# Root sums of the grouped norm computed inside the attention, tokens on partitions

## Chip, cores and metric

The kernel runs on one core of a Trainium2 chip. The metric is the device time in microseconds of the execution.

## What is computed

One layer of a hybrid model on 576 tokens: 512 of a prompt and 8 sequences of 8 sampled tokens. A projection of the normed input gives z, the convolution input, the step sizes, q, k, v and two gates. A state-space scan and a windowed attention with sinks run on them, their outputs are gated, merged and projected, and a product-key expert network follows. The change concerns the norm of the scan's output, by groups of 256 channels (8 groups), for each token:

```
y = y.reshape(bsz, l, SSM_D_INNER) * jax.nn.silu(z.astype(f32))
yg = y.reshape(bsz, l, SSM_N_GROUPS, SSM_D_INNER // SSM_N_GROUPS)
yg = yg * lax.rsqrt(jnp.mean(yg * yg, axis=-1, keepdims=True) + NORM_EPS)
y = (yg.reshape(bsz, l, SSM_D_INNER) * lw['ssm_norm_w'].astype(f32)).astype(z.dtype)
return y @ lw['w_ssm_out'], conv_new, ssm_new.astype(ssm_prev.dtype)
```

The attention itself does not need this norm, nor does the norm need the attention. Both are needed by the merge behind them.

## The kernel before

Activations lie with channels on the 128 partitions and the 576 tokens along the row (T = 576, HT = 288). Five engines run programs of their own and meet in semaphores. Each weight tile of 128 output channels (1024 x 128, 512 KB) is handled in order everywhere: SyncE loads it into `raw`, ScalarE's `high` rounds it into `whi` (L1380), GpSimd's `low` subtracts to give `wlo` (L632), and TensorE multiplies three times (hi x hi, hi x lo, lo x hi), here in `project` (L733, both token halves, 48 matmuls) or `gate_raw` (L958, one half, 24 matmuls).

Stages that matter here, by time of the trace: the scan and z (to about 550 us), q, k and v (to 628), the attention (628 to 794), the projection of the attention output with the grouped norm beside it (795 to 865), the projection of the scan's output (from 865), and the rest.

The attention has UA = 20 units: 16 of the prompt (4 token chunks by 4 key heads) and 4 of the samples. The orders are written out by hand, one list for each engine:

- TensorE, for u = 0 to 19: `turn(u)` (L1063, waits for the normalised weights), `scores(u + 2)` (L1046), `gate_half(u)`, then `values(u)` (L1090; L1077 and L1079 for samples). `gate_half(u)` is half a weight tile of the output gates, unrelated to the attention, one half tile in every unit. It waits in `ga_used` until ScalarE has copied half tile u - 1 out of bank 7.
- ScalarE: `take(u)` (L1593, L1594), `weights(u + 2)` (L1581, the exponentials), `store_gate(u)` (L1602 copies the half tile into `rinv`, L1604 sends it to memory). Where u is odd, `store_gate` ends in `high` for the weight tile that `gate_half(u + 3)` needs.
- VectorE: `back(u + 1)` (L2196 to L2199), `take` of two units together where u is even (L2218, L2219), `front(u + 2)` (L2182, L2158 to L2162), which ends in the maxima that `weights(u + 2)` waits for.
- GpSimd: `low` for each weight tile, one for two units.

In the next stage there are 8 projections. Around each, one group of the norm is done: ScalarE squares two tiles (`z_square`, L1633), TensorE multiplies them with a 128 x 128 matrix of ones, which leaves the sum of squares on all 128 partitions (`group_sums`, L1124), ScalarE takes the root of 128 x 576 elements (`z_std`, L1640), VectorE takes the reciprocal (`yn`, L2244), scales the two tiles (L2248) and splits them (L2257, L2258). Between, `att` (L1887) applies the attention's gate. TensorE's order is `group_sums(0)`, tile 0, `group_sums(1)`, tile 1, and so on.

Of the kernel before, what the change touches and what calls it, by code (L numbers as in the profile page):

```python
# [22 lines left out]
F32 = mybir.dt.float32  # L23
# [7 lines left out]
P = 128  # L31
# [176 lines left out]
def build(nc, xT, wt, pu, pv, consts, params, subk, conv_in, ropes, amask, smask, s_in, kct, kc, vc,  # L208
# [3 lines left out]
    act_dram = nc.dram_tensor("activations", [ET, P, DT], F32).ap()  # L212
    ga_dram = nc.dram_tensor("gates_raw", [GS_E + GT_N, P, T], F32).ap()
# [3 lines left out]
    with ctx:  # L217
# [53 lines left out]
        RW = put(misc, "row_weight", [P, ROWS])  # L271
        tmp_at = misc[0]
# [85 lines left out]
        SQZ = [nc.alloc_sbuf_tensor_at(f"sqz{i}", [P, T], F32, offset=conv_at + 2304 * i) for i in range(2)]  # L358

# [52 lines left out]
        def sem(name):  # L412
# [8 lines left out]
        abc_in = [sem(f"abc_in{i}") for i in range(4)]  # L421
        acum_copied, acum_out, e2_in, e2_ready = [
            sem(n) for n in ("acum_copied", "acum_out", "e2_in", "e2_ready")]
# [23 lines left out]
        dt_v, dt_abs, dt_exp, dt_ready, dtt_ready, dtk_ready = [  # L447
            sem(n) for n in ("dt_v", "dt_abs", "dt_exp", "dt_ready", "dtt_ready", "dtk_ready")]
# [12 lines left out]
        rs_ready, rope_done, v_ready, v_turned, v_tok = [  # L461
            sem(n) for n in ("rs_ready", "rope_done", "v_ready", "v_turned", "v_tok")]
# [7 lines left out]
        zs_ready, yz_ready, zsq_ready, zsq_used, zstd, yn_done = [  # L470
            sem(n) for n in ("zs_ready", "yz_ready", "zsq_ready", "zsq_used", "zstd", "yn_done")]
# [19 lines left out]
        def _(sp):  # L491
# [17 lines left out]
            def load_rows(u):  # L509

                c, g = divmod(u, NG)
                src = acum_dram[c:c + 1, 4 * g:4 * g + 4, :].to_broadcast([P, 4, P])
                sp.dma_start(ABC[u % 4][:, :, :], src).then_inc(abc_in[u % 4], 16)

            def load_rows_sample(s):

                if s < 2:
# [3 lines left out]
                    .then_inc(abc_in[s], 16)  # L521
# [14 lines left out]
            sp.wait_ge(acum_out, 16 * NC)  # L536
# [88 lines left out]
        def _(pool):  # L625
# [71 lines left out]
            with pool.Fori((N_QKV + 3) // 2, N_GU // 2) as i:  # L697
                for k in range(2):
                    low(Idx(k, i, 2))
# [20 lines left out]
        def _(pe):  # L720
# [407 lines left out]
            group_sums(0, first=True)  # L1128
            pe.wait_ge(o_done, UNITS // 2 + SB // 2)
            for k in range(2):  # L1130
                project(Idx(N_ATT + k), Idx(P_ATT + k), OH, OL)
                group_sums(k + 1)
            with pe.Fori(1, KD // 2 - 1) as i:
                for k in range(2):
                    project(Idx(N_ATT + k, i, 2), Idx(P_ATT + k, i, 2), OH, OL)
                    group_sums(i * 2 + (k + 1))
            for k in range(2):
                project(Idx(N_ATT + KD - 2 + k), Idx(P_ATT + KD - 2 + k), OH, OL)
                if k == 0:
                    group_sums(KD - 1)  # L1140
# [200 lines left out]
        def _(act):  # L1341
# [105 lines left out]
            for c in range(NC):  # L1447
                t0, L = chunk(c)
                act.dma_start(acum_dram[c, :, 0:L], ACT_[:, t0:t0 + L]).then_inc(acum_out, 16)
# [27 lines left out]
            def exps(u):  # L1477
# [3 lines left out]
                act.wait_ge(abc_in[u % 4 if u < PU else g // 2], 16 * (u // 4 + 1 if u < PU else NG + 1))  # L1481
# [114 lines left out]
            def store_gate(u):  # L1596
# [3 lines left out]
                act.wait_ge(ga_out[h], 16 * (GS_E + m))  # L1600
                cut = RINV[:, h * HT:(h + 1) * HT]
# [1114 lines left out]
```

## Time and profile before

| | us |
|---|---|
| runs | 2532.62, 2545.24, 2552.91 |
| median | 2545.24 |
| span of the profiled execution | 2530.3 |
| TensorE busy | 2409.4 (95%) |
| VectorE busy | 1780.0 (70%) |
| ScalarE busy | 1077.0 (43%) |
| GpSimd busy | 886.8 (35%) |

The span runs from the first to the last instruction of one execution. The profile names no separate time for that execution, so the runs stand beside it: the fastest is 2.3 us above the span, the median 14.9 us. In the rows, PE is TensorE, PEld its weight loads, DVE VectorE, ACT ScalarE, POOL GpSimd. The busy shares are means over stages that differ; the rows below come from the two stages of the change. PEclk is the granted clock of TensorE, 1.00 being 2.4 GHz and 0.50 being 1.2 GHz.

### The profile page before, as it was taken

How to read it: one execution, taken by the hardware profiler on the slowest of the kernel's cores; microseconds unless marked ns; L12 is line 12 of the kernel's file. 1: busy time of each engine (PE TensorE's matmuls, PEld its weight loads, DVE VectorE, ACT ScalarE, POOL GpSimd, SP SyncE). 2: the span in 40 equal slices, each digit the busy share in tenths (PEclk: the TensorE clock that was granted, in tenths of full speed). 3: DMA queues.
4: the chain of work that ended last, by engine and by line, in shares of the span. 5: the costliest groups of instructions: out<-in, count | busy, mean ns of one | idle time of the engine just before them, and what ended most of it. 6: DMA issues, size and time to landing. Idle time of an engine off the chain costs nothing.

```text
span 2530.3 us, 44965 instructions
## 1 busy us (share of the span) xinstructions
PE 2409.4 (95%) x15016; PEld 2231.8 (88%) x15016; DVE 1780.0 (70%) x3445; ACT 1077.0 (43%) x2049; POOL 886.8 (35%) x504
## 2 busy tenths in 40 slices
PE   7999779999799999899999999999999999999997
PEld 6999659989678999899998899899899999999996
DVE  6655775543664822377999887788568888888887
ACT  3554763335554522133343677777532222222222
POOL 1333364433111343244455543444423331222221
PEclk8999999999998999999999999999999999999998
DMA  3222344432211323133444788899999999999994
GB/s 140 75 82 75 110 136 158 156 116 84 78 58 62 100 88 121 58 106 121 143 153 146 247 325 318 301 345 355 339 324 317 321 314 307 311 312 310 310 309 148
DMA packets 271272, 498.46 MB, mean 197 GB/s; under 512 B 138000, under 2 KB 176912, under 8 KB 270096
## 3 DMA queue, kind: packets, MB, share of 16 engines
q1 hardware_dynamic: 71472, 228.49, 26.7%
q10 hardware_dynamic: 162816, 134.23, 16.3%
q0 software_dynamic: 36864, 134.23, 15.2%
q8 instruction: 63, 1.03, 0.2%
q14 instruction: 57, 0.47, 0.1%
HBM read 421.13 MB, written 76.93 MB: 197 GB/s over the span
## 4 chain that ended last, share of the span: by engine, by line
PE 57%; issue 23%; DVE 10%; POOL 4%; ACT 3%; DMA 2%; ACTq 1%; DVEq 0%; POOLq 0%; SPq 0%
PE ps L1295 24%; PE ps L1190 14%; PE ps L733 9%; PE ps L918 5%; POOL wlo L632 4%; PE ps L1260 3%; DMA raw<-wt 1%; DVE seg L2035 1%; PE ps L886 1%; DVE onehot_pick L2420 1%; ACT whi L1380 1%; PE ps L901 1%; ACT rinv L1778 1%; DVE expert_parts L2426 1%; DVE onehot_pick L2423 1%
## 5 line engine op out<-in xcount | busy, mean ns | idle before, releaser
L1380 ACT ACTIVATE whi<-raw 128x1024 fp32r<-128x1024 f32 x373 | 394.4, 1058 | 1069.9 <-PE ps L1295 452.9
L632 POOL TENSOR_TENSOR wlo<-raw,whi 128x1024 fp32r<-128x1024 f32 x177 | 439.0, 2481 | 842.2 <-ACT whi L1380 842.2
L1190 PE MATMUL ps<-h_hi,whi 128*128 128x448 f32 x1024 | 381.3, 372 | 5.8 <-DVE wlo L2481 4.9
L1190 PE MATMUL ps<-h_hi,wlo 128*128 128x448 f32 x1024 | 375.5, 367 | 0.0
L1190 PE MATMUL ps<-h_lo,whi 128*128 128x448 f32 x1024 | 375.3, 367 | 0.0
L1295 PE MATMUL ps<-act_hi,whi 128*128 128x448 f32 x1000 | 365.2, 365 | 0.0
L1295 PE MATMUL ps<-act_lo,whi 128*128 128x448 f32 x1000 | 365.2, 365 | 0.0
L1295 PE MATMUL ps<-act_hi,wlo 128*128 128x448 f32 x1000 | 365.2, 365 | 0.0
L2481 DVE TENSOR_TENSOR wlo<-raw,whi 128x1024 fp32r<-128x1024 f32 x196 | 240.3, 1226 | 157.2 <-ACT whi L1380 142.8
L643 POOL DMA_INDIRECT row<-pv,row_idx x128 | 166.2, 1298 | 465.8 <-DVE row_acc L2509 442.1
L643 POOL DMA_INDIRECT row<-pu,row_idx x128 | 185.8, 1451 | 251.4 <-DVE row L2472 231.9
L1190 PEld LDWEIGHTS ps<-h_hi,whi 128*128 128x128 f32 x1024 | 193.2, 189 | 23.1 <-issue 5.0
L1190 PEld LDWEIGHTS ps<-h_hi,wlo 128*128 128x128 f32 x1024 | 192.9, 188 | 16.5
L1190 PEld LDWEIGHTS ps<-h_lo,whi 128*128 128x128 f32 x1024 | 193.2, 189 | 15.1
L1295 PEld LDWEIGHTS ps<-act_hi,wlo 128*128 128x128 f32 x1000 | 187.8, 188 | 14.9
L1295 PEld LDWEIGHTS ps<-act_lo,whi 128*128 128x128 f32 x1000 | 187.8, 188 | 14.9
L1295 PEld LDWEIGHTS ps<-act_hi,whi 128*128 128x128 f32 x1000 | 187.8, 188 | 14.9
L733 PE MATMUL ps<-h_hi,whi 128*128 128x288 f32 x832 | 181.7, 300 | 11.6 <-POOL wlo L632 11.6
L733 PE MATMUL ps<-h_hi,wlo 128*128 128x288 f32 x832 | 180.4, 299 | 0.0
L733 PE MATMUL ps<-h_lo,whi 128*128 128x288 f32 x832 | 180.2, 299 | 0.0
L2509 DVE SCALAR_TENSOR_TENSOR row_acc<-row,row_weight,row_acc 128x1024 f32<-128x1024 f32 x128 | 163.7, 1279 | 0.5 <-DVE row_acc L2509 0.3
L2472 DVE SCALAR_TENSOR_TENSOR row<-row,h_rows 128x1024 f32<-128x1024 f32 x128 | 151.8, 1220 | 3.0 <-DMA row<-pu,row_idx 3.0
(344 smaller groups left out, 4773.7 us busy)
## 6 DMA issues: line engine op xcount, KB each, us to landing
raw<-wt SPq DMA_DIRECT2D x245, 512.0 KB
raw<-pv SPq DMA_DIRECT2D x128, 512.0 KB
activations<-tmp ACTq DMA_DIRECT2D x128, 224.0 KB
gates_dense<-g_block ACTq DMA_DIRECT2D x7, 4096.0 KB
g_tile<-gates_dense ACTq DMA_DIRECT2D x128, 224.0 KB
gelu<-activations ACTq DMA_DIRECT2D x128, 224.0 KB
a_cum_rows<-decay_sums SPq DMA_DIRECT2D x32, 256.0 KB, 3.1
state_s<-s_in SPq DMA_DIRECT2D x16, 512.0 KB, 6.0
```

The source lines that it names most:

```text
L632: pool.tensor_tensor(lo, raw[n.par][:, :], hi.bitcast(F32), ALU.subtract).then_inc(split_ready, 1)
L643: pool.indirect_dma_start(GR[b][:, :], None, table[:, :], bass.IndirectOffsetOnAxis(ap=IDX[:, s:s + 1], axis=0))\
L733: mm = pe.matmul(PS[2 * p.par + h][:, 0:HT], w[slot][:, k, :], x[:, k0 + k + (l0 if x is xl else 0), h * HT:(h + 1) * HT], start=first and ...
L886: mm = pe.matmul(bank(PU + g)[:, lo:lo + SL], S0[v % 8][:, b, :], UBS[:, NG + g, SL * b:SL * (b + 1)], start=True, stop=True)
L918: mm = pe.matmul(PS[2 + h][:, 0:HT], w[slot][:, k, :], x[:, k, h * HT:(h + 1) * HT], start=k == 0 and i == 0, stop=k == KD - 1 and i == 2)
L1190: mm = pe.matmul(PS[2 * p.par][:, 0:DT], w[slot][:, k, :], x[:, k, 0:DT], start=k == 0 and w is whi and x is HH, stop=k == KD - 1 and w is ...
L1260: mm = pe.matmul(out, OJ[k][:, q, :], AI[k][:, q, :], start=True, stop=True)
L1295: mm = pe.matmul(PS[d][:, 0:DT], w[s][:, d, :], x[b][:, :], start=first and w is whi and x is ACH, stop=False)
L1380: act.activation(whi[slot][:, :, :].rearrange("p k c -> p (k c)"), raw[slot][:, :], ACT.Copy)\
L2472: dve.scalar_tensor_tensor(row[:, :], row[:, :], 1.0, HS[:, :], ALU.mult, ALU.mult, accum_out=dot).then_inc(row_used, 1)
L2481: dve.tensor_tensor(lo, raw[slot][:, :], hi.bitcast(F32), ALU.subtract).then_inc(split_ready, 1)
L2509: dve.scalar_tensor_tensor(ACCS[:, :], GR[b][:, :], w, ACCS[:, :], ALU.mult, ALU.add).then_inc(row_used, 1)
```

## The change

Squares, sums and roots move into the attention. After `store_gate(u)`, for u = 0 to 15, ScalarE squares one tile. GpSimd adds the two squares of a group behind its `low` of that pair of units. TensorE, ahead of `gate_half(2g + 2)`, multiplies the sum (as the stationary operand, 5 chunks of 128 tokens) with one column of ones, so the sums of all groups come out as 5 x 8 columns with tokens on partitions, in the free part of bank 7. At unit 17 one root of 128 x 40 elements is taken, VectorE takes one reciprocal, and after the attention TensorE turns the 40 columns into rows. ScalarE copies them and sends them to memory in 5 DMAs; from there each group's row comes back, repeated over 128 partitions, by one DMA into one of two buffers (`RB`). In the projection stage the sums of TensorE, the roots of ScalarE and the wide reciprocals of VectorE are gone. Two semaphores are renamed (`abc_in` to `bcast_in`, `acum_out` to `rows_out`).

```diff
+    zinv_dram = nc.dram_tensor("group_roots", [NG, T], F32).ap()
...
+        ZINV = put(misc, "group_root", [P, NC, NG])
+        ZROW = put(misc, "group_root_rows", [NC * NG, P])
...
+        RB = [nc.alloc_sbuf_tensor_at(f"group_rinv{i}", [P, T], F32, offset=conv_at + 2304 * i) for i in range(2)]
...
-            with pool.Fori((N_QKV + 3) // 2, N_GU // 2) as i:
+            with pool.Fori((N_QKV + 3) // 2, (N_GT + 1) // 2) as i:
+                for k in range(2):
+                    low(Idx(k, i, 2))
+            low(Idx(N_GT + 1))
+            for g in range(NG):
+                low(Idx(N_GT + 2 + g))
+                pool.wait_ge(zsq_ready, 2 * g + 2)
+                pool.tensor_tensor(SQZ[1][:, :], SQZ[1][:, :], SQZ[0][:, :], ALU.add).then_inc(zsq_added, 1)
+            low(Idx(N_GT + 2 + NG))
+            with pool.Fori((N_GT + 3 + NG) // 2, N_GU // 2) as i:
                 for k in range(2):
                     low(Idx(k, i, 2))
...
+                if u % 2 == 0 and 0 < u <= 2 * NG:
+                    group_sum(u // 2 - 1)
                 gate_raw(Idx(N_GT + m), h, PS[3 if u == GA_AT else 7], (ga_half, tile_done)[h])
+
+            def group_sum(g):
+
+                pe.wait_ge(zsq_added, g + 1)
+                for c in range(NC):
+                    t0 = min(c * P, T - P)
+                    mm = pe.matmul(PS[7][:, HT + NG * c + g:HT + NG * c + g + 1], SQZ[1][:, t0:t0 + P], ONES[:, 0:1],
+                                   start=True, stop=True)
+                mm.then_inc(zsq_used, 1)
 
             gate_half(GA_AT)
             pe.wait_ge(v_tok, 1)
@@ -1114,30 +1138,15 @@
...
+            pe.wait_ge(zinv_ready, 1)
+            pe.transpose(PS[4][0:NC * NG, 0:P], ZINV[:, :, :].rearrange("p c g -> p (c g)"), ident).then_inc(pt_ready, 1)
             pe.wait_ge(sc_used, UA)
-            def group_sums(g, first=False):
-                pe.wait_ge(zsq_ready, g * 2 + 2)
-                if not first:
-                    pe.wait_ge(zstd, g)
-                for k in range(2):
-                    for h in range(2):
-                        mm = pe.matmul(PS[4 + h][:, 0:HT], ONES[:, :], SQZ[k][:, h * HT:(h + 1) * HT],
-                                       start=k == 0, stop=k == 1)
-                    mm.then_inc(zsq_used, 1)
-
-            group_sums(0, first=True)
             pe.wait_ge(o_done, UNITS // 2 + SB // 2)
             for k in range(2):
                 project(Idx(N_ATT + k), Idx(P_ATT + k), OH, OL)
-                group_sums(k + 1)
-            with pe.Fori(1, KD // 2 - 1) as i:
+            with pe.Fori(1, KD // 2) as i:
                 for k in range(2):
                     project(Idx(N_ATT + k, i, 2), Idx(P_ATT + k, i, 2), OH, OL)
-                    group_sums(i * 2 + (k + 1))
-            for k in range(2):
-                project(Idx(N_ATT + KD - 2 + k), Idx(P_ATT + KD - 2 + k), OH, OL)
-                if k == 0:
-                    group_sums(KD - 1)
...
+                if u == UA - 3:
+                    act.wait_ge(zsq_used, NG)
+                    act.activation(ZINV[:, :, :].rearrange("p c g -> p (c g)"), PS[7][:, HT:HT + NC * NG], ACT.Sqrt, bias=Q[:, Q_EPS:Q_EPS + 1],
+                                   scale=float(NG) / INNER).then_inc(zstd, 1)
...
+            def z_square(g, k):
+
+                if g == 0:
+                    act.wait_ge(rope_done, 10)
+                    act.wait_ge(yz_ready, CI)
+                elif k == 0:
+                    act.wait_ge(zsq_added, g)
+                else:
+                    act.wait_ge(zsq_used, g)
+                act.activation(SQZ[k][:, :], at(UX, g * 2 + k), ACT.Square).then_inc(zsq_ready, 1)
...
+                if u < CI:
+                    z_square(u // 2, u % 2)
...
-            def z_square(g, k, first=False):
-                if not first:
-                    act.wait_ge(zsq_used, g * 2 + (k - 1))
-                act.activation(SQZ[k][:, :], at(UX, g * 2 + k), ACT.Square).then_inc(zsq_ready, 1)
-
-            def z_std(g, first=False):
-                act.wait_ge(zsq_used, g * 2 + 2)
-                if not first:
-                    act.wait_ge(y_scaled, g)
-                for h in range(2):
-                    ins = act.activation(RINV[:, h * HT:(h + 1) * HT], PS[4 + h][:, 0:HT], ACT.Sqrt,
-                                         bias=Q[:, Q_EPS:Q_EPS + 1], scale=float(NG) / INNER)
-                ins.then_inc(zstd, 1)
-
+            def rinv_back(g, k):
+
+                act.dma_start(RB[k][:, :], zinv_dram[g:g + 1, :].to_broadcast([P, T]) if isinstance(g, int) else
+                              zinv_dram[bass.ds(g, 1), :].to_broadcast([P, T])).then_inc(bcast_in[k], 16)
+
+            act.wait_ge(pt_ready, UA + 1)
+            act.activation(ZROW[:, :], PS[4][0:NC * NG, 0:P], ACT.Copy).then_inc(pt_copied, 1)
+            act.wait_ge(pt_copied, UA + 1)
+            for c in range(NC):
+                t0, L = chunk(c)
+                act.dma_start(zinv_dram[:, t0:t0 + L], ZROW[c * NG:(c + 1) * NG, P - L:P]).then_inc(rows_out, 16)
...
-                z_std(m, first=first and k == 0)
                 if not (first and k == 0):
                     high(plus(n, 1))
                 if not (last and k):
-                    for j in range(2):
-                        z_square(m + 1, j)
                     if not (first and k == 0):
+                        act.wait_ge(y_scaled, m)
+                        rinv_back(m + 1, 1 - k)
                         p = plus(p, -1)
                         act.wait_ge(slot_used[p.par], p.half + 1)
                     gate_back(m + (GS_B + 1), 1 - k)
...
+            act.wait_ge(rows_out, 16 * 2 * NC)
             for k in range(2):
-                z_square(0, k, first=True)
+                rinv_back(k, k)
...
+                if u == UA - 2:
+                    dve.wait_ge(zstd, 1)
+                    dve.reciprocal(ZINV[:, :, :], ZINV[:, :, :]).then_inc(zinv_ready, 1)
...
-            def yn(g, yh):
-                dve.wait_ge(zstd, g + 1)
-                own.link(dve.reciprocal(RINV[:, :], RINV[:, :]))
+            def yn(i, b, yh):
+                g = i * 2 + b
+                dve.wait_ge(bcast_in[b], i * 16 + 16 * (NG + 2))
                 for k in range(2):
                     y = at(UX, g * 2 + k)
                     m = g * 2 + k
                     ins = dve.scalar_tensor_tensor(y, y, Q[:, bass.ds(m + Q_SNW, 1)],
-                                                   RINV[:, :], ALU.mult, ALU.mult)
+                                                   RB[b][:, :], ALU.mult, ALU.mult)
```

## Rows read from the trace of the kernel before

**Rows 1.** Windows of stages: us, busy by engine (instructions), PEclk, DMA share, GB/s.

```profile
688.00:703.00 15.00, 13.04 (x98) 10.44 (x97) 10.01 (x21) 8.00 (x26) 2.40 (x1) 1.00 0.16 56
748.00:760.00 12.00, 12.00 (x142) 10.07 (x141) 8.59 (x25) 7.38 (x20) 3.26 (x2) 1.00 0.26 82
806.30:864.50 58.20, 58.20 (x394) 55.23 (x392) 54.67 (x62) 42.20 (x54) 16.00 (x7) 1.00 0.28 85
```

**Rows 2.** Timeline of TensorE in the attention: start, us, operation, [idle before].

```profile
695.39 0.40 PE L958 MATMUL ps<-h_hi,whi 128*128 128x288 f32 x1 [1.65 <-ACT rinv L1602]
...
702.26 0.40 PE L958 MATMUL ps<-h_hi,whi 128*128 128x288 f32 x1 [0.31 <-ACT rinv L1602]
...
705.61 1.08 PE L1090 MATMUL ps<-p_turned,v_tok 128*64 128x256 f32 x8
...
707.65 1.14 PE L1046 MATMUL ps<-k_pad,q 64*128 64x256 f32 x8
...
747.39 0.40 PE L958 MATMUL ps<-h_hi,whi 128*128 128x288 f32 x1 [0.54 <-ACT rinv L1602]
...
759.45 0.40 PE L958 MATMUL ps<-h_hi,whi 128*128 128x288 f32 x1
```

**Rows 3.** Timeline of ScalarE in the attention.

```profile
701.82 0.39 ACT L1602 ACTIVATE rinv<-ps 128x288 f32<-128x288 f32 x1
...
702.68 1.06 ACT L1380 ACTIVATE whi<-raw 128x1024 fp32r<-128x1024 f32 x1 [0.47 <-ACT rinv L1602]
...
707.92 0.51 ACT L1581 ACTIVATE scores<-scores,att_small 128x256 f32<-128x256 f32 x1 [3.22 <-DVE att_small L2162]
```

**Rows 4.** Timeline of GpSimd in the attention.

```profile
703.81 2.40 POOL L632 TENSOR_TENSOR wlo<-raw,whi 128x1024 fp32r<-128x1024 f32 x1 [12.65 <-ACT whi L1380]
...
759.14 2.40 POOL L632 TENSOR_TENSOR wlo<-raw,whi 128x1024 fp32r<-128x1024 f32 x1 [7.79 <-ACT whi L1380]
```

**Rows 5.** Timeline of VectorE in the attention.

```profile
704.82 1.28 DVE L2182 TENSOR_TENSOR scores<-ps,mask_prompt 128x512 f32<-128x512 f32 x2
```

**Rows 6.** Groups of GpSimd instructions by shape: busy us, mean ns.

```profile
L716 POOL TENSOR_TENSOR y_out<-y_out,rinv 128x576 f32<-128x576 f32 x2 | 3.3, 1654 | 23.9 <-DVEq L2584 23.9
```

**Rows 7.** Timeline of TensorE, small float32 matmuls of the sample units.

```profile
790.55 0.30 PE L1077 MATMUL ps<-p_turned,v_cache 128*64 128x32 f32 x2
...
794.00 0.30 PE L1079 MATMUL ps<-p_turned,v_tok 64*64 64x32 f32 x2
```

**Rows 8.** Timeline of TensorE behind the gap at 552.8 us.

```profile
558.37 0.84 PE L733 MATMUL ps<-h_hi,whi 128*128 128x288 f32 x2 [5.54 <-POOL wlo L632]
```

**Rows 9.** Windows of TensorE behind three gaps; PEclk is the granted clock.

```profile
558.30:561.80 3.50, 3.43 (x14) 3.44 (x15) 3.47 (x5) 1.56 (x3) 1.82 (x1) 0.50 0.47 150
640.60:643.60 3.00, 2.98 (x14) 2.48 (x16) 1.56 (x3) 2.52 (x8) 0.47 (x1) 0.50 0.57 188
710.00:714.00 4.00, 3.56 (x16) 3.56 (x17) 3.70 (x6) 1.47 (x4) 0.00 (x0) 0.61 0.13 41
```

**Rows 10.** Timeline of TensorE in the attention output projection.

```profile
796.25 3.85 PE L1124 MATMUL ps<-sqz,ones 128*128 128x288 f32 x8 [1.95 <-ACT sqz L1633]
799.71 0.64 PE L733 MATMUL ps<-o_hi,whi 128*128 128x288 f32 x2
...
806.32 2.10 PE L1124 MATMUL ps<-sqz,ones 128*128 128x288 f32 x8
808.04 0.64 PE L733 MATMUL ps<-o_hi,whi 128*128 128x288 f32 x2
...
879.99 0.53 PE L733 MATMUL ps<-y_hi_a,whi 128*128 128x288 f32 x2 [1.01 <-POOL wlo L632]
```

**Rows 11.** Groups of the output projection, 794.9 to 882 us.

```profile
L2244 DVE RECIPROCAL rinv<-rinv 128x576 f32<-128x576 f32 x8 | 30.0, 3746 | 6.1 <-ACT rinv L1640 6.1
```

**Rows 12.** DMA issues by tile: KB each, median us to landing.

```profile
a_cum_rows<-decay_sums SPq DMA_DIRECT2D x32, 256.0 KB, 3.1
...
decay_sums<-a_cum_by_head ACTq DMA_DIRECT2D x4, 16.0 KB, 3.0
```

More of the change, by code:

```diff
@@ L420, in build @@
         s0_moved = [sem(f"s0_moved{i}") for i in range(8)]
-        abc_in = [sem(f"abc_in{i}") for i in range(4)]
-        acum_copied, acum_out, e2_in, e2_ready = [
-            sem(n) for n in ("acum_copied", "acum_out", "e2_in", "e2_ready")]
+        bcast_in = [sem(f"bcast_in{i}") for i in range(4)]
+        acum_copied, rows_out, e2_in, e2_ready = [
+            sem(n) for n in ("acum_copied", "rows_out", "e2_in", "e2_ready")]
         cache_in = [sem(f"cache_in{i}") for i in range(SB // 2)]
@@ L445, in build @@
         dve_own = sem("dve_own")
-        dt_v, dt_abs, dt_exp, dt_ready, dtt_ready, dtk_ready = [
-            sem(n) for n in ("dt_v", "dt_abs", "dt_exp", "dt_ready", "dtt_ready", "dtk_ready")]
+        dt_abs, dt_exp, dt_ready, dtt_ready, dtk_ready = [
+            sem(n) for n in ("dt_abs", "dt_exp", "dt_ready", "dtt_ready", "dtk_ready")]
         conv_done, silu_done = sem("conv_done"), sem("silu_done")
@@ L459, in build @@
         dup_in = sem("dup_in")
-        rs_ready, rope_done, v_ready, v_turned, v_tok = [
-            sem(n) for n in ("rs_ready", "rope_done", "v_ready", "v_turned", "v_tok")]
+        rs_ready, rope_done, v_turned, v_tok = [
+            sem(n) for n in ("rs_ready", "rope_done", "v_turned", "v_tok")]
         blk_staged, sc_ready, m_ready, p_exp, p_ready = [
@@ L469, in build @@
         z_half = sem("z_half")
-        zs_ready, yz_ready, zsq_ready, zsq_used, zstd, yn_done = [
-            sem(n) for n in ("zs_ready", "yz_ready", "zsq_ready", "zsq_used", "zstd", "yn_done")]
+        zs_ready, yz_ready, zsq_ready, zsq_added, zsq_used, zstd, zinv_ready, yn_done = [
+            sem(n) for n in ("zs_ready", "yz_ready", "zsq_ready", "zsq_added", "zsq_used", "zstd", "zinv_ready", "yn_done")]
         merged = sem("merged")
@@ L520, in load_rows_sample @@
                 sp.dma_start((ABC[:2] + ASR)[s][0:NS, :, :].rearrange("p a (b t) -> p (a b) t", b=2), src)\
-                    .then_inc(abc_in[s], 16)
+                    .then_inc(bcast_in[s], 16)
             def load_states(v):
@@ L534, in spread @@
                 sp.dma_start(BTK[NS:P, 2 * q:2 * q + 2, :], BTK[0:NS, 2 * q:2 * q + 2, :]).then_inc(dup_in, 16)
-            sp.wait_ge(acum_out, 16 * NC)
+            sp.wait_ge(rows_out, 16 * NC)
             for u in range(4):
@@ L2266, in att_pair @@
                     if half:
-                        yn(m, lambda j: at(YHB, (i * 2 + (k - KD // 2)) * 2 + j))
+                        yn(i, k, lambda j: at(YHB, (i * 2 + (k - KD // 2)) * 2 + j))
                     else:
-                        yn(m, lambda j: at(YHA, m * 2 + j))
+                        yn(i, k, lambda j: at(YHA, m * 2 + j))
                     att(Idx(N_ATT + k, i, 2), Idx(P_ATT + k, i, 2), m, k)
@@ L2275, in _ @@
                 with dve.Fori(first, last) as i:
-                    own.enter(i, first, 12)
+                    own.enter(i, first, 10)
                     att_pair(i, half)
```

7 lines of the change are left out of this document (3 added, 4 removed).

## Prediction

> **What bounds the kernel now.** I read the share of busy time first (TensorE 95%), then windows of the two stages that the change touches, then the timelines of each engine in them. In the middle of the attention, TensorE is busy 13.04 of 15 us, VectorE 10.01, ScalarE 8.00, GpSimd 2.40 [rows 1]: no engine is full, so a loop of waits sets the pace. GpSimd's long waits end in the same place in each turn, and two units take 15.05 us (the copy of an odd half tile starts at 701.82, the one before it 15.05 earlier, the next 15.05 later). The loop is VectorE's `front`, then ScalarE's exponentials, then VectorE's `back`. TensorE waits 1.65 us in one unit and 0.31 in the other, each time for the copy of the last half tile [rows 2], and ScalarE has 3.22 us free ahead of the exponentials [rows 3]. From 748 us on, in the last prompt units and the samples, TensorE is busy 12.00 of 12 us [rows 1] and bounds. In the output projection it is busy 58.20 of 58.20 us, VectorE 54.67 [rows 1].
>
> **What the change removes.** In the projection stage the first sum holds TensorE from the end of the attention's last matmul at 794.30 to 799.71: a wait of 1.95 for the squares and 3.46 for the sum at half clock [rows 10]. With the sums gone the first projection waits for the last split of the attention's output only, some 0.7 us, and for one small transpose, 0.2. It starts near 795.2, 4.5 us earlier. The half clock passes to the projection: 3.4 us at half speed do 1.7 us of work, so 1.7 is lost again. The other seven sums cost 1.72 each (806.32 to 808.04) [rows 10]: 12.0 us. Behind the stage, TensorE waits 1.01 at 879.99 [rows 10] for a weight tile that came late because VectorE was late with the last group; I count 1.0 as saved. Sum: 4.5 - 1.7 + 12.0 + 1.0 = 15.8 us.
>
> What is late next there? VectorE: without eight reciprocals of 3.75 [rows 11], the 54.67 us of seven steps become 28.4, or 4.1 in a step of 6.61 (799.71 to 806.32) [rows 10]. It has room. ScalarE loses squares, wide roots and changes of tables, and gains one DMA issue a step. The new DMA of group m + 1 is issued in the step of tile m and used a step later: 3.1 us for the nearest transfer of its kind [rows 12] lies inside 6.61. Only the start is tight. Transpose, copy and five issues end near 797; small rows to memory land 3.0 later, the repeated row 3.1 after that [rows 12]: 803.3. The first group then takes VectorE 4.1 us and `att(0)` 0.8: 808.2. TensorE needs that for its third tile at 795.2 + 1.7 + 2 x 6.61 = 810.1. So it is free by 1.9 us, and each microsecond beyond costs one.
>
> **What it adds in the attention.** 16 squares on ScalarE, 0.7 us each, fall into 3.22 free us [rows 3] in one unit and about 2.9 in the other: nothing while they are short. But the chain of a group runs through four queues. At an odd unit, ScalarE copies the half tile (701.82), issues its DMA, and runs `high` from 702.68 to 703.74 [rows 3]. GpSimd's `low` runs from 703.81 to 706.21 [rows 4], and the new addition is queued behind it. Its inputs have been ready since 704.4, so GpSimd's order, not the squares, sets its start. The addition of 128 x 576 is not in the trace. Scaled from 2.40 for 1024 columns it is 1.35, and an addition-like operation of the same shape took 1.65 [rows 6]; I take 1.45. The sum is ready at 707.7, 5.9 us after the copy began. TensorE has stood in `group_sum` since 702.26, where before it began `gate_half` [rows 2]. Behind this wait in its queue are the half tile, `values(2g)`, `turn(2g + 1)` and `scores(2g + 3)`, and the last of them is what VectorE's `front(2g + 3)` waits for. Before, those scores were ready at 708.79 and wanted by VectorE at 711.7: 2.9 us of room, and the delay is larger.
>
> The five matmuls of a sum are float32, two passes each. The small float32 calls of the samples take 0.234 each (16 of them from 790.55 to 794.30) [rows 7], which gives 1.17. By passes of the old sums (eight in 1.72) it would be 2.15 [rows 10]; the moving part here is one column, so I take 1.17.
>
> Now the wait closes a loop. From the copy of one odd half tile to the next: 5.9 to the end of the addition, 1.2 for the sum, 3.35 for the half tile (702.26 to 705.61), 3.2 for values, turn and scores (705.61 to 708.79) [rows 2], 3.1 for `front` (704.82 to 707.9) [rows 5], 2.1 for the exponentials, then the copy. That is 18.8 us for two units, against 15.05: 3.7 more. It holds for the waits ahead of `gate_half` 4 to 12, five times: 18.5. The wait at 2 costs nothing, as its `low` was queued before the attention began. The last two lie where TensorE is full. At 747.39 `gate_half(14)` began [rows 2]; now it begins at 746.94 + 5.9 + 1.2 = 754.0, 6.6 later. `gate_half(16)` began at 759.45 [rows 2]; its `low` starts at 759.14 [rows 4], so the addition ends at 763.0, the sum at 764.1: 4.6 later. Total at full clock: 18.5 + 6.6 + 4.6 = 29.7 us.
>
> The clock adds to this. Each new wait leaves TensorE idle for some 4.6 us. Behind an idle stretch of 5.54 [rows 8] the granted clock was 0.50, that is 1.2 GHz, for the next 3.5 us, and behind one of 3.47 it was 0.50 as well; behind 1.65 it was 0.61 in one pair of units [rows 9] and 1.00 in most [rows 1]. 4.6 lies between the two that fell. The half clock then covers the sum and the first half of the half tile, which is on the loop: 3.5 us at half speed lose 1.75. Seven times that is 12.2, which makes 41.9. Since short gaps went both ways I count five falls of seven: 8.8, so 38.5 us.
>
> The Trainium skill, TensorE: Matmul & The Clock Gate, part 1 (the clock gate), says that the reduced clock is the resting state and that only sustained activity releases it. By that rule all seven waits would be followed by half clock, which would be the upper sum; the trace agrees for the two long gaps above.
>
> Net: 38.5 - 15.8 = +22.7 us. The root of 40 columns and the reciprocal lie beside TensorE's sample work and cost nothing; if that cover failed, they would cost under 2 us. The profiled span of 2530.3 becomes 2553. The median of the runs is 14.9 above that span, and I add the difference to the median: 2545.2 + 22.7 = 2568.
>
> **The rivals.** (A) *The wait is hidden*, and the kernel gets faster. The mechanism would be the slack of TensorE in the attention: 1.65 + 0.31 us in two units [rows 2] and 2.9 us of early scores. It decides at the point where the sum is added no later than some 3 us after the copy; then only the 1.2 us sums count where TensorE is full (2 x 1.2 = 2.4), and the result is -15.8 + 2.4, about 2532. It would need GpSimd to reach the addition without the 2.40 us subtraction in front, and its queue order speaks against that. 0.08.
>
> (B) *The wait costs, the clock doesn't fall.* +29.7 - 15.8 = +13.9: 2559. For it speak the many gaps under 2.6 us that kept the clock; against it, both longer ones. 0.27.
>
> (C) *All dear.* The clock falls each time (41.9), the addition takes 1.65 and the sums 2.15, so each of seven turns has 1.2 more (8.4), less some overlap with the slow clock; and the rows come back 2 us too late at the start. +41.9 + 6 + 2 - 15.8 = +34: 2579. 0.17.
>
> (D) *It doesn't do what it says*: the norm's rows gate the projection, because the trip to memory and back takes over 3 us more than the 6.1 counted in every step. The stage would keep its 58 us, and about 12 of the 15.8 be lost: 2580. The step is 6.61 with one transfer in it, so 0.03.
>
> **How the numbers follow.** The forecast (five falls) has 0.45, A 0.08, B 0.27, C 0.17, D 0.03. The range leaves out A and the far end of C and D, and takes in B with a few us of the runs' own spread (20 us from lowest to highest): 2551 to 2585. A measurement of this kernel tells about 1% (25.5 us) from no change. Faster by over 1% would need more than all that is removed: 0.02. Slower by over 1% are D, nearly all of C and some two fifths of the forecast's own case, whose spread reaches both sides of +25.5: 0.38. Within 1%: 0.60.
>
> **What would show it.** In the changed profile: turns of two units of 18.5 to 20.5 us from the fourth unit on, TensorE idle for 4 to 5 us ahead of the new one-column matmuls with GpSimd's addition named as releaser, granted clock near 0.5 behind it, and the attention some 30 to 42 us longer. Then eight projections at 6.6 us each with no break, and the scan's projection in full step at once. I am wrong if the addition runs before the subtraction's end, if the five matmuls take much over 2 us, or if TensorE stops before the third projection.

## The result and the profile after

The changed kernel takes 2572.49 us (median of 4 runs, 2568.95 to 2575.43) against 2538.93 before (4 runs, 2532.39 to 2552.91). The ratio is 1.0141, 95% interval 1.0108 to 1.0173: slower by 1.4%. Later runs of the kernel before had medians of 2531.5 to 2534.3, so the real difference is nearer 38 to 41 us than 33.6. The two profiled spans, 2530.3 and 2569.8, differ by 39.5.

I cut both executions at the same three places: the start of VectorE's copy into `q_sample` (the attention begins), the start of the last split of the attention's output, and the start of the first matmuls of the scan's projection. The rows of the changed kernel's timeline, of VectorE and TensorE:

```profile
627.60 0.43 DVE L2173 COPY q_sample<-q 128x512 f32<-128x512 f32 x1
...
844.97 0.29 DVE L2230 TENSOR_TENSOR o_lo<-ps,o_hi 128x128 fp32r<-128x128 f32 x1
...
902.38 0.51 PE L746 MATMUL ps<-y_hi_a,whi 128*128 128x288 f32 x2 [0.43 <-DVE att L1908]
```

Attention: 844.97 - 627.60 = 217.4 us. Output projection: 902.38 - 844.97 = 57.4. The same cuts in the kernel before:

```profile
631.21 0.43 DVE L2152 COPY q_sample<-q 128x512 f32<-128x512 f32 x1
...
794.66 0.29 DVE L2209 TENSOR_TENSOR o_lo<-ps,o_hi 128x128 fp32r<-128x128 f32 x1
...
865.39 0.51 PE L733 MATMUL ps<-y_hi_a,whi 128*128 128x288 f32 x2 [0.67 <-issue]
```

That gives 163.5 and 70.7. So the attention grew by 53.9 us (38.5 predicted) and the stage behind it lost 13.3 (15.8 predicted). The sum, 40.6, covers the whole difference of the spans.

Why the attention grew is seen best in one turn of two units. Here is TensorE of the changed kernel. In [rows 2] the half tile of this place in the turn began after a wait of 0.31 us:

```profile
698.15 2.27 PE L1122 MATMUL ps<-ones,sqz 128*128 128x1 f32 x10 [4.58 <-POOL sqz L708]
...
706.23 1.08 PE L1103 MATMUL ps<-p_turned,v_tok 128*64 128x256 f32 x8
...
708.27 1.13 PE L1059 MATMUL ps<-k_pad,q 64*128 64x256 f32 x8
```

GpSimd in the same turn, to be held against [rows 4]:

```profile
694.29 2.35 POOL L636 TENSOR_TENSOR wlo<-raw,whi 128x1024 fp32r<-128x1024 f32 x1 [17.36 <-ACT whi L1389]
696.61 1.39 POOL L708 TENSOR_TENSOR sqz<-sqz,sqz 128x576 f32<-128x576 f32 x1
```

And ScalarE, against [rows 3]:

```profile
692.30 0.39 ACT L1615 ACTIVATE rinv<-ps 128x288 f32<-128x288 f32 x1
...
694.12 0.67 ACT L1630 ACTIVATE sqz<-u_x 128x576 f32<-128x576 f32 x1
...
706.34 0.41 ACT L1615 ACTIVATE rinv<-ps 128x288 f32<-128x288 f32 x1 [5.76 <-PE ps L971]
```

Read them together. The copy of the odd half tile begins at 692.30. The second square is done at 694.79, but GpSimd first runs the weights' subtraction and ends the addition at 698.00. TensorE has waited 4.58 us for it. From there the sum, the half tile and the values follow one another on TensorE (698.15 to 706.23 and on), and ScalarE's next copy waits 5.76 us for that half tile. The next odd copy comes at 714.64, 22.34 us after this one, where [rows 3] had 15.05.

The waits from 643 to 830 us, which hold all eight sums (engine and line that waited, releaser: us in total, times, longest):

```profile
DVE scores L2203 <- PE ps L1059: 36.4, 6, 7.2
PE ps L1122 <- POOL sqz L708: 34.9, 8, 4.8
```

The eight sums wait 34.9 us, and VectorE's `front` waits for scores queued behind them. Behind each of these gaps the granted clock is near half. Windows that begin at the sum (us, busy by engine, PEclk, DMA share, GB/s):

```profile
655.40:662.80 7.40, 7.29 (x34) 7.16 (x34) 4.41 (x10) 2.17 (x9) 0.00 (x0) 0.57 0.01 2
698.00:706.20 8.20, 8.05 (x34) 7.92 (x34) 1.91 (x6) 2.17 (x9) 0.00 (x1) 0.51 0.16 61
741.90:748.70 6.80, 6.72 (x34) 6.66 (x34) 1.84 (x6) 2.17 (x9) 0.00 (x0) 0.62 0.20 71
763.00:771.10 8.10, 8.07 (x35) 7.92 (x35) 1.80 (x5) 2.17 (x9) 0.00 (x0) 0.51 0.16 59
```

This is the 1.2 GHz level for 5 to 8 us, where the prediction, from [rows 9], counted 3.5. The other four gaps are like these: read in windows of one microsecond, the stretches at 0.50 behind the eight sums add up to 51 us, which is 25.6 us of work not done. Outside these windows the attention's matmuls have their full-clock durations again: values 1.08 and scores 1.13 above, as in [rows 2].

In the output projection the eight wide sums are gone. TensorE's stops there:

```profile
860.55 0.54 PE L746 MATMUL ps<-o_hi,whi 128*128 128x288 f32 x2 [0.36 <-DVE att L1908]
...
867.49 0.54 PE L746 MATMUL ps<-o_hi,whi 128*128 128x288 f32 x2 [0.28 <-DVE att L1908]
...
874.42 0.54 PE L746 MATMUL ps<-o_hi,whi 128*128 128x288 f32 x2 [0.28 <-DVE att L1908]
```

A tile takes 6.93 us (867.49 to 874.42) and not the 8.33 of [rows 10] with its sum, but TensorE does stop, each time for `att`. VectorE shows why:

```profile
853.68 1.55 DVE L2272 SCALAR_TENSOR_TENSOR u_x<-u_x,params_sb,group_rinv 128x576 f32 x2 [8.43 <-DMA group_rinv<-group_roots]
...
862.08 0.46 DVE L2281 CAST y_hi_a<-u_x  x1
...
863.25 2.66 DVE L2281 CAST y_hi_a<-u_x  x1
...
866.62 0.81 DVE L1908 TENSOR_TENSOR att<-ps,tmp 128x288 f32 x2
```

The same cast takes 0.46 us once and 2.66 the next time. In the second one GpSimd's subtraction is running:

```profile
862.62 2.96 POOL L636 TENSOR_TENSOR wlo<-raw,whi 128x1024 fp32r<-128x1024 f32 x1 [5.14 <-ACT whi L1389]
```

It ends at 865.58 and the cast at 865.91.

### The profile page after: what moved, and what is told of

Read it like the earlier page. It is cut to its first block, busy times and chain, and to the rows that moved or that the text cites. A ratio compares the mean times of both kernels' runs of the same rounds, so it can differ in the third digit from the quotient of the medians.

```text
span 2569.8 us, 44934 instructions
## 1 busy us (share of the span) xinstructions
PE 2422.5 (94%) x15033; PEld 2248.9 (88%) x15033; DVE 1770.1 (69%) x3438; ACT 1054.1 (41%) x2021; POOL 895.6 (35%) x512
## 4 chain that ended last, share of the span: by engine, by line
PE 56%; issue 17%; DVE 13%; ACT 6%; POOL 4%; DMA 3%; ACTq 1%; DVEq 0%; POOLq 0%; SPq 0%
PE ps L1304 23%; PE ps L746 11%; PE ps L1199 9%; PE ps L931 4%; POOL wlo L636 3%; PE ps L971 2%; DMA raw<-wt 2%; ACT whi L1389 2%; PE ps L1269 1%; DMA activations<-tmp 1%; ACT rinv L1799 1%; DVE seg L2056 1%; DVE onehot_pick L2444 1%; PE ps L899 1%; DVE expert_parts L2450 1%
## 5 line engine op out<-in xcount | busy, mean ns | idle before, releaser
L647 POOL DMA_INDIRECT row<-pv,row_idx x128 | 160.5, 1254 | 471.5 <-DVE row_acc L2533 447.8
```

The costliest lines, as they stand in the source:

```text
L647: pool.indirect_dma_start(GR[b][:, :], None, table[:, :], bass.IndirectOffsetOnAxis(ap=IDX[:, s:s + 1], axis=0))\
```

## The experiments

My theory: the addition, queued behind the subtraction, closes a loop through TensorE's queue; the half clock behind each gap multiplies it; squares and sums themselves cost nothing. Rivals: the sums' own work costs the time; the clock has little part in it; one-column matmuls are what keeps the clock low. Lengths are measured by the three cuts above, each from one profile. Two of the kernels (e1_late, e6_att_first) have the same order throughout the attention and still differ by 2.1 us there, and e10_rows_early, which differs in the last unit only, by 2.2 more, so a few us between two lengths tell nothing:

| kernel | attention, us | against before | projection, us | ratio of times [95%] |
|---|---|---|---|---|
| before | 163.5 | | 70.7 | |
| after | 217.4 | +53.9 | 57.4 | 1.0141 [1.0108, 1.0173] |
| e4_no_wait | 163.6 | +0.1 | 57.2 | 0.9959 [0.9934, 0.9984] |
| e1_late | 170.6 | +7.1 | 56.9 | 0.9978 [0.9948, 1.0008] |
| e2_warm | 191.3 | +27.8 | 57.1 | 1.0077 [1.0049, 1.0104] |
| e3_pe_adds | 194.4 | +30.9 | 56.9 | 1.0053 [1.0031, 1.0075] |
| e8_add_first | 200.1 | +36.6 | 56.9 | 1.0098 [1.0067, 1.0128] |
| e9_one_sum | 204.8 | +41.3 | 57.0 | 1.0115 [1.0062, 1.0169] |
| e6_att_first | 168.5 | +5.0 | 53.0 | 0.9967 [0.9937, 0.9997] |
| e10_rows_early | 166.3 | +2.8 | 53.0 | 0.9940 [0.9913, 0.9968] |

**The work without the wait (e4_no_wait).** The matmuls of a sum read the ones and no longer the squares, so TensorE waits for nothing; ScalarE waits for the additions once, ahead of the rows' copy. All squares, additions and matmuls stay; the sums' values are left out.

```diff
-                pe.wait_ge(zsq_added, g + 1)
...
-                    mm = pe.matmul(..., SQZ[1][:, t0:t0 + P], ONES[:, 0:1],
+                    mm = pe.matmul(..., ONES[:, :], ONES[:, 0:1],
...
+            act.wait_ge(zsq_added, NG)
```

> The small matmuls stay in their place but multiply the ones, which are always ready, in place of the sum of squares, so TensorE has no wait for the addition (the norm is left out of the result in this way: its roots are those of a constant). Squares, additions, roots and transfers all run. Theory: TensorE goes on at once; what is left is 1.2 us for the matmuls where it is full, so about 2530, within 4 us of the kernel with the sums one unit later. Rival (queueing on ScalarE, not TensorE's wait): 2560 to 2575.

It took 2521.67 us against 2534.33. The attention is 163.6 us, the length of the kernel before, and its turns are 15.05 us again. So in the turns the sixteen squares, the eight additions and the small matmuls cost nothing; the growth comes from the wait. Behind 744 us, where TensorE is full, two sums of 1.28 us do add to its work; a higher clock hid them in this profile (0.91 over 757 to 775 us, 0.80 in the kernel before over 760 to 777). What is left is the gain of the stage behind.

**The sum one unit later (e1_late).** Nothing is left out; the same sum stands ahead of the next unit's half tile, when its addition is long done.

```diff
-                if u % 2 == 0 and 0 < u <= 2 * NG:
-                    group_sum(u // 2 - 1)
+                if u % 2 and 3 <= u <= 2 * NG + 1:
+                    group_sum((u - 3) // 2)
```

> The sum of group g is placed ahead of half tile 2g + 3 in TensorE's order, one unit later than in the change; all other work is the same. Theory (the wait for the addition stands in TensorE's queue ahead of the half tile, and the half clock follows from it): the addition has long ended, TensorE doesn't idle for it, two units return to 15 to 15.5 us, the attention is 3 to 6 us longer than before the change, and the time is 2528 to 2534, against 2538.9 before and 2572.5 changed. Rival (the work itself costs: 16 squares in ScalarE's queue and the small matmuls): the work is all still there, so the time stays at 2560 to 2575.

2526.22 us, not to be told from the kernel before (the interval holds 1); the turns are 15.05. TensorE at the sums of groups 2, 3 and 7 (group 2 is the one shown of the changed kernel at 698.15):

```profile
690.62 1.28 PE L1122 MATMUL ps<-ones,sqz 128*128 128x1 f32 x10 [0.35 <-ACT rinv L1615]
...
705.67 1.28 PE L1122 MATMUL ps<-ones,sqz 128*128 128x1 f32 x10 [0.91 <-ACT rinv L1615]
...
766.25 2.29 PE L1122 MATMUL ps<-ones,sqz 128*128 128x1 f32 x10
```

1.28 us at full clock, and the wait ahead of it is the old one for the half tile's copy; the last one, at half clock, has no wait ahead of it. The attention is still 7.1 us longer than before. The surplus lies in the last third. e1_late's windows of it:

```profile
757.00:775.00 18.00, 18.00 (x132) 16.28 (x132) 7.15 (x20) 5.42 (x19) 3.34 (x2) 0.72 0.11 38
775.00:797.00 22.00, 22.00 (x149) 19.29 (x149) 1.75 (x6) 4.36 (x9) 4.69 (x2) 0.80 0.13 45
```

TensorE is never idle there, yet the granted clock is 0.72 and 0.80. The kernel before had 0.80 and 0.90 in its 760 to 777 and 777 to 794, and e4_no_wait 0.91 and 0.90. Some of the 7 us is thus clock in one execution: e6_att_first, with the same order in the attention, has 168.5 us at a mean clock of 0.91 where e1_late has 0.89, and e10_rows_early 166.3 at 0.94. How much of the rest the sums cause was not tried.

**Keep the wait, keep the clock (e2_warm).** 34 matmuls on tiles that are in place anyway, into the bank that the half tile overwrites, run in the gap ahead of each sum.

```diff
+                    slot = slot_of(Idx(N_GT + m))
+                    pe.wait_ge(split_ready, N_GT + m + 1)
+                    for j in range(34):
+                        pe.matmul(PS[7][:, 0:HT], whi[slot][:, j % KD, :], HH[:, j % KD, 0:HT], start=True, stop=True)
                     group_sum(u // 2 - 1)
```

> The changed kernel with 34 matmuls of no use (288 columns, results overwritten) between TensorE's arrival and its wait for the addition, about 4.5 us of work at full clock, so that TensorE is busy and not idle while it waits; the wait itself stays. Theory: the granted clock stays near 1.0 behind it, the sum falls from 2.27 to 1.2 us and the half tile from 4.5 to 5.9 down to 3.35, so each of eight turns gives back 2.3 to 3.6 us: about 2550, turns of 18.5 to 19. Rival (the clock is not on the loop, or the fillers only push the end out): 2570 to 2580.

2555.94 us. The clock holds and the sum takes 1.28. The window of one turn from the sum on, and its sum in a later turn:

```profile
692.70:698.60 5.90, 5.90 (x47) 5.57 (x47) 3.01 (x7) 2.20 (x10) 1.23 (x1) 1.00 0.27 92
```

```profile
712.73 1.28 PE L1126 MATMUL ps<-ones,sqz 128*128 128x1 f32 x10
```

The turns are 18.7 us, the number that the prediction's loop gave at full clock (18.8). The attention is 27.8 us longer than before and 26.1 shorter than in the changed kernel. So in these profiles the 53.9 split into 27.8 for the wait (29.7 predicted) and 26.1 for the clock (8.8 predicted). The split is rougher than it looks. The profiled execution is the fastest of e2_warm, 13.8 us below its median, and by the medians the fillers gave back only 16.6 us (2572.49 to 2555.94). The clock of its attention is also higher (0.97) than in the kernel before (0.93), so the fillers took away half clock that the change had not brought. For the larger figure speak the 25.6 us read from the changed kernel's own windows. Either way the clock cost about twice what was predicted, or three times.

The Trainium skill, TensorE: Matmul & The Clock Gate, part 1, in "HAM oscillation — how this bites in real kernels", says that a kernel whose matmul bursts are each followed by a wait pays the cold start once for each burst. The changed kernel's trace agrees: eight gaps, eight falls, and the time comes back when the gaps are filled.

**No addition at all (e3_pe_adds).** TensorE adds the two squares in its accumulator: ten matmuls a group and no GpSimd.

```diff
-                pool.tensor_tensor(SQZ[1][:, :], SQZ[1][:, :], SQZ[0][:, :], ALU.add).then_inc(zsq_added, 1)
...
-                pe.wait_ge(zsq_added, g + 1)
+                pe.wait_ge(zsq_ready, 2 * g + 2)
...
+                    for k in range(2):
+                        mm = pe.matmul(..., SQZ[k][:, t0:t0 + P], ONES[:, 0:1], start=k == 0, stop=k == 1)
```

> No addition on GpSimd: TensorE accumulates both squares of a group (10 matmuls in place of 5), in the place where the change has its sum, and waits for ScalarE's second square only. Theory: the wait ends about 3.3 us earlier, the gap is under 2 us and seldom lowers the clock; the doubled matmuls take 2.3 us. Turns of 16.5 to 17.5, time 2540 to 2550. Rival (the small matmuls are what costs): twice as many make it slower than the change, 2585 or more. Rival (GpSimd's addition is innocent, the squares come late): 2570.

2548.58 us, ratio 1.0053. TensorE at one sum, and windows from the sum on:

```profile
691.31 2.88 PE L1121 MATMUL ps<-ones,sqz 128*128 128x1 f32 x20 [1.37 <-ACT sqz L1629]
```

```profile
691.30:699.80 8.50, 8.49 (x44) 8.50 (x44) 4.84 (x10) 3.01 (x11) 1.74 (x1) 0.60 0.20 64
711.00:718.20 7.20, 7.17 (x46) 7.03 (x48) 4.72 (x10) 3.03 (x11) 1.74 (x1) 0.76 0.25 75
```

The gap is only 1.37 us in most turns, and the clock still falls in every turn. The turns last 17.7 to 19.8 us against 16.5 to 17.5 expected. The prediction's idea that gaps under 2.6 us keep the clock doesn't hold here. But the fall comes later than in the changed kernel, when the sum is already running:

```profile
691.30:692.80 1.50, 1.49 (x14) 1.50 (x14) 1.50 (x3) 0.83 (x2) 1.50 (x1) 1.00 0.04 11
692.80:699.80 7.00, 7.00 (x32) 7.00 (x32) 3.34 (x8) 2.17 (x9) 0.24 (x1) 0.51 0.23 75
```

Whether the short gap or the twenty small passes bring it here was not separated. The second square is still on the loop, since ScalarE makes it behind the copy and `high`, and a sum of twenty passes adds its own length.

**The addition ahead of the subtraction (e8_add_first).** Only GpSimd's order changes.

```diff
-                low(Idx(N_GT + 2 + g))
                 pool.wait_ge(zsq_ready, 2 * g + 2)
                 pool.tensor_tensor(SQZ[1][:, :], SQZ[1][:, :], SQZ[0][:, :], ALU.add).then_inc(zsq_added, 1)
+                low(Idx(N_GT + 2 + g))
```

> The changed kernel with GpSimd's addition ahead of its subtraction of the pair instead of behind it. Theory (the sum is late because the subtraction of 2.35 us stands in front of the addition in GpSimd's queue): the addition starts with the second square, some 1.7 us earlier; TensorE's gap falls from 4.6 to 2.9 us and each of eight turns by 1.7, and the clock falls as before: 2556 to 2562. If the shorter gap spares the clock in half of the turns: 2545. Rival (the subtraction is wanted as early): no gain, 2572.

2553.31 us; the attention is 17.3 us shorter than in the changed kernel.

```profile
753.54 2.26 PE L1122 MATMUL ps<-ones,sqz 128*128 128x1 f32 x10 [2.85 <-POOL sqz L707]
```

```profile
694.90:702.50 7.60, 7.59 (x36) 7.44 (x36) 3.85 (x8) 2.17 (x9) 2.17 (x1) 0.55 0.23 71
```

The gap shrinks from 4.6 to 2.85 us, so the subtraction was part of it, as said. The half clock stays in most turns: 0.55. The first gap is unchanged (3.59 against 3.60), and seven gaps shorter by 1.74 us make 12.2 of the 17.3. Most of the rest is clock: behind the eight sums it was low for 43 us in all against 51, and behind the last, a gap of 1.73, it did not fall:

```profile
791.61 1.25 PE L1122 MATMUL ps<-ones,sqz 128*128 128x1 f32 x10 [1.73 <-POOL sqz L707]
```

**One matmul for five (e9_one_sum).** One call of forty columns takes the place of the five of one column; four of the five chunks of a group's sum are left out.

```diff
-                for c in range(NC):
-                    t0 = min(c * P, T - P)
-                    mm = pe.matmul(PS[7][:, HT + NG * c + g:HT + NG * c + g + 1], SQZ[1][:, t0:t0 + P], ONES[:, 0:1],
-                                   start=True, stop=True)
+                mm = pe.matmul(PS[7][:, HT:HT + NC * NG], SQZ[1][:, 0:P], ONES[:, 0:NC * NG], start=True, stop=True)
```

> The changed kernel with one small matmul in place of five for each group, behind the same wait (the sums of four of the five chunks of tokens, and the right column of each group, are left out, so the norm is not that of the reference). It tells the wait and the clock from the small matmuls. Theory: gap stays at 4.6 us; 0.45 us of small matmuls at half clock in place of 2.27 saves 1.8 in each of eight turns, 14 us, so 2558. If the one-column matmuls also kept the clock down (the half tile behind them took 4.5 to 5.9 us against 3.35 at full clock), the half tile is shorter here by another 0.5 us or more a turn, with half clock over about 3.5 us behind the gap: 2552. If neither matters: 2572.

2557.67 us, attention 12.6 us shorter.

```profile
689.93 0.62 PE L1120 MATMUL ps<-ones,sqz 128*128 128x40 f32 x2 [4.58 <-POOL sqz L708]
```

```profile
689.90:695.90 6.00, 5.97 (x28) 5.84 (x28) 1.79 (x5) 2.17 (x9) 0.00 (x0) 0.56 0.22 84
```

The gap is the same 4.58. Dense wide matmuls stand right behind it, and the clock is 0.56 over 6.0 us. So a gap of this length needs no small matmuls to bring the half clock. Whether they prolong it stays open: from the sum on it lasted 5.0 us here, on the mean of eight, and 6.4 in the changed kernel, but part of that is the sum itself, and turns vary (3.4 to 5.8 and 5.1 to 7.9). The saving is mostly their own length, 2.27 against 0.62 a group, 13.2 us over eight.

**Order of `att` (e6_att_first).** On top of e1_late, VectorE reads a tile of the projection before it scales the next group.

```diff
+                    att(Idx(N_ATT + k, i, 2), Idx(P_ATT + k, i, 2), m, k)
                     yn(...)
-                    att(Idx(N_ATT + k, i, 2), Idx(P_ATT + k, i, 2), m, k)
```

> The sums one unit later as in the first experiment, and in the projection stage VectorE applies the attention's gate to tile m ahead of the scaling and splitting of group m, not behind it. In the changed kernel's stage one cast of 0.46 us takes 2.65 beside GpSimd's subtraction in every step, VectorE's step becomes 6.93 us, and TensorE stops 0.3 us ahead of each tile for the gate. Theory (that order is what TensorE waits for): the waits ahead of tiles 3 to 8 go, the stage is 2 us shorter (55 in place of 57.3 us), and the time is 2 us below that of the first experiment: about 2524. Rival (the last group is now split later, and the scan's projection waits for it): the same time as the first experiment or 1 to 3 us more.

2521.77 us. The stops ahead of the projection's tiles vanish (projection 53.0 us), but the last group is late for the scan's second tile:

```profile
860.73 0.53 PE L746 MATMUL ps<-y_hi_b,whi 128*128 128x288 f32 x2 [3.48 <-DVE y_lo L2282]
```

To the second tile it takes 63.0 us against e1_late's 63.4. The stop had moved. So had VectorE's blocked instruction:

```profile
807.03 3.67 DVE L2272 SCALAR_TENSOR_TENSOR u_x<-u_x,params_sb,group_rinv 128x576 f32 x2
```

The two scalings take 3.67 us where they take 1.55 undisturbed; the cast behind them has its 0.46.

**Rows sent earlier (e10_rows_early).** On top of e1_late, the transpose, the roots' copy and the five writes move into the last unit, ahead of its last half tile's copy.

```diff
+                if u == UA - 1:
+                    pe.wait_ge(zinv_ready, 1)
+                    pe.transpose(PS[7][0:NC * NG, HT:HT + P], ZINV[:, :, :].rearrange("p c g -> p (c g)"), ident)
...
-            pe.wait_ge(zinv_ready, 1)
-            pe.transpose(PS[4][0:NC * NG, 0:P], ZINV[:, :, :].rearrange("p c g -> p (c g)"), ident).then_inc(pt_ready, 1)
...
+                if u == UA - 1:
+                    act.activation(ZROW[:, :], PS[7][0:NC * NG, HT:HT + P], ACT.Copy).then_inc(zinv_ready, 1)
+                    act.wait_ge(zinv_ready, 2)
+                    for c in range(NC):
+                        t0, L = chunk(c)
+                        act.dma_start(zinv_dram[:, t0:t0 + L], ZROW[c * NG:(c + 1) * NG, P - L:P]).then_inc(rows_out, 16)
```

> The first experiment (sums one unit later), and the turning of the roots into rows and their way to memory are moved from the end of the attention to its last unit, behind the last half tile's wait, into free columns of bank 7; the order in the projection stage is the old one. In the first experiment VectorE stood 7.9 us for the first repeated row (it arrived 7.9 us after the attention's last split), then needed 6.93 us a step, and TensorE stopped about 0.3 us ahead of tiles 3 to 8. Theory (the stage is bound by VectorE from the moment at which the first row comes): the first group starts 4 us sooner, TensorE's stops vanish, and the projection stage takes 55 us in place of 57.3, the time 2 us less than in the first experiment: ratio to before 0.997, about 2525 where before is at 2533. Rival (a step of 6.93 us by itself holds TensorE, whatever the start): TensorE's stops return and the stage stays at 57.

2517.80 us, ratio 0.9940: the lowest median of the study, and nothing is left out. Its interval overlaps that of e6_att_first. VectorE's first group:

```profile
800.15 1.55 DVE L2273 SCALAR_TENSOR_TENSOR u_x<-u_x,params_sb,group_rinv 128x576 f32 x2 [5.10 <-DMA group_rinv<-group_roots]
```

That is 5.1 us after the last split ends; in the changed kernel it was 8.4. From 795.15 on TensorE has no stop up to the scan's second tile, each tile takes 6.40 us, and the second tile comes 59.4 us after the last split, against 63.9 in the changed kernel and 77.7 before. The block is still there, but it has left the casts for the scalings, which take 3.07 to 3.31 us for two in every later step. VectorE's step is 6.4 us in place of 6.93, and its first group starts 3.3 us earlier than in the changed kernel. Which of the two removes the stops was not separated.

## Why the prediction was right in sign and short in size

The prediction said 2568 us in 2551 to 2585; the median is 2572.49. That nearness owes something to the base. The three runs shown had a median of 2545.2, while the kernel before is near 2533 in the later runs. The difference of the spans was predicted as 22.7 and is 39.5. The signs named ahead tell the same: turns of 18.5 to 20.5 us were 21.1 to 22.3 in the prompt units, an attention 30 to 42 us longer was 53.9 longer, the five matmuls of a sum took 2.27 us, and TensorE did stop before the third projection (0.36 us at 860.55).

- **The loop: right in its mechanism.** The additions wait behind `low`, TensorE stands in `group_sum`, scores come late, `front` waits. The turn at full clock was worked out as 18.8 us, and e2_warm has 18.7. The addition was taken as 1.45 and is 1.39; the wait as 4.6 and is 4.58.
- **"The wait at 2 costs nothing": wrong, but small.** Its addition starts as soon as its square is there:

```profile
653.09 2.28 POOL L708 TENSOR_TENSOR sqz<-sqz,sqz 128x576 f32<-128x576 f32 x1 [11.21 <-ACT sqz L1630]
...
655.51 2.26 PE L1122 MATMUL ps<-ones,sqz 128*128 128x1 f32 x10 [3.60 <-POOL sqz L708]
```

  The subtraction in front was indeed gone, but copy, square and an addition of 2.28 us make a gap of 3.60 all the same. The first turn is 3.1 us longer (33.71 against 30.60 for four units).
- **The wait as a whole: 27.8 us measured (e2_warm), 29.7 predicted.** By the medians it is about 35 (e2_warm is 21.6 us above the kernel before, and its next stage saves 13.6). The 3.7 us a turn hold (18.7 against 15.05). The prediction priced seven waits, and the eighth, at 2, is the small one above.
- **The clock: the step that failed.** "I count five falls of seven: 8.8" took 3.5 us of half speed a fall, from [rows 9]. The window there was shorter than the stretch: in the kernel before the clock stayed at the half level for 5.7 us behind the gap of 5.54, to 564.1, and for 5.2 us behind the gap of 3.47.

```profile
561.80:564.00 2.20, 2.20 (x11) 2.20 (x10) 1.37 (x1) 0.00 (x0) 0.76 (x1) 0.50 0.14 34
```

  So both terms were too small, the length and the count. The count rested on the gaps under 2.6 us that kept the clock; but [rows 10] has a gap of 1.95 with the half clock behind it, which the prediction itself reads so. In the changed kernel the clock fell in all eight, and stayed low for 5 to 8 us: 698.15 to about 706 in the turn shown. 7.8 us at half speed do 3.9 us of work. The 26.1 us that e2_warm's profile gave back are 3.3 for each of eight falls, which is 6.5 us at half speed; the windows show 6.4 on the mean. The sum, the whole half tile and the first values lie under it, and all of them are on the loop, so little hides the loss. Even the prediction's upper case (C) took 1.75 a fall.
- **Sums at 1.17 us: 1.28 warm**, as in e1_late, but 2.27 in each turn of the changed kernel, at half clock. The rate from [rows 7] was right for the full clock.
- **Squares and sums hidden: right in the turns** (e4_no_wait), with two sums of 1.28 us in the full part.
- **The stage, -15.8 predicted, -13.3 to the scan's first tile and -13.8 to its second.** The start and the lost sums came as said (TensorE starts 0.4 us after the last split). The 1.0 us counted as saved behind the stage did not come, the weight tile is as late as before:

```profile
916.35 0.54 PE L746 MATMUL ps<-y_hi_a,whi 128*128 128x288 f32 x2 [0.95 <-POOL wlo L636]
```

  "VectorE has room" failed: its step was taken as 4.1 us of 6.61 by leaving out 3.75 of reciprocal. Without the reciprocal, GpSimd's subtraction falls on the casts, and one cast of each step takes 2.40 to 2.66 us. What the reciprocal cost was in part paid again. The start was sized well: `yn(0)` began at 853.68, 8.7 us after the last split began, where the prediction had 803.3 - 794.66 = 8.6. But its first cast took 2.45 us and not 0.46, and this 2.0 is all of "free by 1.9 us". From there VectorE's step of 6.9 leaves it late by 0.3 us at each tile. An unbroken tile takes 6.40 (e10_rows_early), so a step of 6.93 costs 0.53 a tile. e10_rows_early, with earlier rows, has none of it.
- **Rivals.** (A), a hidden wait, fell with the first gap. (B), a clock that doesn't fall, is e2_warm's case: +13.9 said, +21.6 by the medians and +10.0 by the spans. (C) had the right reason with the wrong length. (D), rows that gate the stage, held for the first group only.

## What to carry to other kernels

A wait that is put at the head of a queue in a loop that is not full costs what exceeds the slack of the work queued behind it: here 3.7 us a turn at full clock, for a gap of 4.6 and a sum of 1.3. Move it one unit back, where its input is old, and the same work is nearly free (e1_late against the changed kernel: 2526 and 2572 us). When such a wait idles TensorE, add the clock to its price, for as long as the half level lasts in the rows (a window that ends sooner hides part of it), and on every turn: here it nearly doubled the cost by the profiles, and added about half again by the medians. And when a long instruction is taken from VectorE, look at what GpSimd runs at that time: here the conflict then fell on the next short one.

## What the runs showed of the hardware

- A gap of 1.37 us ahead of the sum was followed by clocks of 0.60 and 0.76 (e3_pe_adds), while [rows 9] and [rows 1] have gaps of 1.65 with 0.61 and 1.00, and a gap of 1.73 was followed by 1.00 (e8_add_first, 791.61). The length of a gap alone didn't tell whether the clock falls.
- In the sample units TensorE was busy 18.00 of 18 us and was still granted 0.72 (e1_late). Small matmuls follow each other there; a busy engine isn't always at the full level.
- A cast into `y_hi_a` takes 0.46 us on VectorE, and 2.66 while GpSimd's subtraction of 128x1024 runs. Before the change the subtraction ran beside the reciprocal, and the casts kept their length:

```profile
845.19 3.75 DVE L2244 RECIPROCAL rinv<-rinv 128x576 f32<-128x576 f32 x1
```

```profile
845.18 2.40 POOL L632 TENSOR_TENSOR wlo<-raw,whi 128x1024 fp32r<-128x1024 f32 x1 [6.42 <-ACT whi L1380]
```

  The Trainium skill, SBUF — State Buffer, in "Who interferes with whom", says that VectorE and GpSimd share one pair of ports, that a cast can be among the instructions that take it, and that the engine which comes second is blocked for the whole instruction of the first. The rows agree: the cast that began at 863.25 ended 0.33 us after the subtraction. With another order of VectorE's queue (e6_att_first) the same delay fell on the scalings, 3.67 us for two.
- GpSimd's addition took 1.39 us in most turns and 2.28 in the first one, at 653.09.
